# One added wait on the load queue of a two-layer attention and mixture-of-experts kernel

## The reference

```python
for l in range(DEPTH):                      # DEPTH = 2
    h = rmsnorm(x, norm_attn[l])
    proj = h @ w_in[l]                      # 1024 x 6336, float32
    ...                                     # three attentions out_a, out_b, out_c
    x = x + mixed.astype(x.dtype) @ w_out[l]
    x = x + hier_moe(rmsnorm(x, norm_ffn[l]), ...)   # silu(t @ w_gate) * (t @ w_up), then @ w_down
return rmsnorm(x, norm_final)
```

## Time and profile before

| | us |
|---|---|
| median of 3 runs | 1009.46 (1009.01 to 1010.76) |
| profiled execution, its own time | 1008.15 |
| its span, first to last instruction | 1006.4 |
| what lies around the span | 1.75 |
| PE busy | 931.0 (93%) |
| the first layer's last right half lands | 497.1 |
| barrier between the layers passed | about 503.6 |

### The profile page before, as it was taken

How to read it: one execution, slowest core, us unless ns; L and a number is a source line. 1 busy time by engine, 2 the same in 40 slices (tenths; PEclk the granted TensorE clock), 3 DMA queues, 4 the chain that set the end, 5 groups by cost and what they waited for, 6 DMA issues and landing times. The chain is left out here.

```text
span 1006.4 us, 13781 instructions
## 1 busy us (share of the span) xinstructions
PE 931.0 (93%) x5372; PEld 613.1 (61%) x5372; DVE 409.6 (41%) x1068; ACT 244.2 (24%) x688; POOL 78.8 (8%) x122
## 2 busy tenths in 40 slices
PE   9999999999999998677899999999999999986676
PEld 8888778775455543334288887887744655531242
DVE  2523676774773211111131337677557621110112
ACT  2211454552111020000111015655411202000002
POOL 0300000104000000000030000000230000000000
PEclk9999999999999999898999999999999999997898
DMA  9985655429889999999998443436398899999995
GB/s 284 302 277 146 145 168 156 168 96 320 336 345 371 421 421 421 421 421 421 363 326 272 136 148 110 142 100 215 123 363 331 340 397 420 420 421 421 421 417 202
DMA packets 133206, 295.06 MB, mean 293 GB/s; under 512 B 14142, under 2 KB 93076, under 8 KB 111636
## 3 DMA queue, kind: packets, MB, share of 16 engines
q1 hardware_dynamic: 128832, 289.41, 77.5%
q10 hardware_dynamic: 4308, 4.75, 2.5%
HBM read 291.50 MB, written 2.64 MB: 292 GB/s over the span
## 5 line engine op out<-in xcount | busy, mean ns | idle before, releaser
L1307 PE MATMUL bank<-ring,tail 128*128 128x256 f32 x672 | 156.2, 383 | 0.2
L2323 PE MATMUL bank<-ring,tail 128*32 128x512 f32 x896 | 112.4, 659 | 47.1 <-DMA ring<-in_moe_w_up 43.1
L1307 PEld LDWEIGHTS bank<-ring,tail 128*128 128x128 f32 x672 | 124.2, 190 | 24.5 <-issue 8.3
L1112 PE MATMUL bank<-tail,ring 128*128 128x256 f32 x512 | 112.6, 380 | 0.0
L2323 PEld LDWEIGHTS bank<-ring,tail 128*32 128x32 f32 x896 | 32.9, 120 | 122.4 <-issue 122.1
L1112 PEld LDWEIGHTS bank<-tail,ring 128*128 128x128 f32 x512 | 96.7, 190 | 13.4 <-issue 0.4
L2669 DVE SCALAR_TENSOR_TENSOR tail<-tail,bank 128x256 f32<-128x256 f32 x16 | 6.7, 421 | 229.5 <-ACT tail L2481 229.5
L1647 ACT ACTIVATE ring<-ring,small 128x128 f32<-128x128 f32 (+1 forms) x128 | 56.6, 443 | 77.5 <-DVE small L1953 77.5
L1469 PE MATMUL bank<-ring,tail 128*128 128x512 f32 x168 | 73.6, 593 | 0.0
L2380 PE MATMUL bank<-ring,tail 128*32 128x512 f32 x480 | 61.5, 623 | 5.6 <-DVE tail L2682 3.6
L2330 PE MATMUL bank<-tail 128*128 128x512 f32 x128 | 59.2, 605 | 0.0
(11 more groups left out here) (350 smaller groups left out, 1205.6 us busy)
## 6 DMA issues: line engine op xcount, KB each, us to landing
ring<-in_moe_w_up SPq DMA_DIRECT2D x56, 1024.0 KB, 21.8
ring<-in_moe_w_gate SPq DMA_DIRECT2D x56, 1024.0 KB, 19.7
ring<-in_moe_w_down SPq DMA_DIRECT2D x52, 1024.0 KB, 14.4
ring<-in_w_in SPq DMA_DIRECT2D x47, 1024.0 KB, 9.5
ring<-in_w_out SPq DMA_DIRECT2D x8, 1024.0 KB, 8.1
ring<-in_moe_w_down SPq DMA_DIRECT2D x16, 512.0 KB, 16.2
ring<-in_moe_w_gate SPq DMA_DIRECT2D x14, 512.0 KB, 9.5
ring<-in_moe_w_up SPq DMA_DIRECT2D x14, 512.0 KB, 9.5
```

The costliest lines, as they stand in the source:

```text
L1112: last = pe.matmul(dst, weight(k), hT[:, k, :], start=(k == 0), stop=(k == KD - 1))
L1307: last = pe.matmul(dst, tokens[:, k, :], weights[:, k, :], start=False, stop=(k == KD // 2 - 1), skip_group_check=True)
L2323: last = pe.matmul(bank[4][CAP * e:CAP * e + CAP, :].rearrange("p (a f) -> p a f", a=2), XT[:, k, CAP * e:CAP * e + CAP], ring[:, lo:hi + ...
```

## The change

One wait is added in `moe_sync`, behind the issues of the eight down halves and ahead of all that follows them on SP. It stands in both layers. No load is added, taken away or put in another order.

```diff
                 down_half(sp, layer, c, 0, landed[moe_slot(c)])
             for c in range(LOADS - 4, LOADS):
                 down_half(sp, layer, c, 1, s_side)
+            sp.wait_ge(s_side, layer * 112 + 112)
             if layer + 1 < DEPTH:
                 sp.wait_ge(s_gu, NGRP - 1)
                 for n in range(EARLY):
```

## The result

The changed kernel takes 1012.92 us at the median of 8 runs (1011.10 to 1016.08), the kernel before 1009.48 (1008.66 to 1011.03) beside it: a ratio of 1.0034 with a 95% interval of 1.0023 to 1.0044, or 3.4 us. (A ratio here is the one measured over the runs and need not be exactly that of the two medians beside it.) A second set of 12 runs of the same kernel gave 1012.44 against 1009.72, 1.0026 (1.0016 to 1.0037). The profiled execution took 1012.67 us with a span of 1010.9, against 1008.15 and 1006.4.

The account below looks back on a forecast made before the run. It took a layer to be PE-bound in attention and bound by the weight stream in its experts. SP's lateness of 1.0 and the clock's 1.4 gave +2.4 on 1009.46, so 1011.9 us, range 1009.4 to 1013.0.

Parts of the forecast that it names:

- SP at the barrier: Seam of the layers: SP's last load issue ends after VectorE, opening the barrier 1.0 us later, bounds 0 to 2.
- SP in time: Rival at the seam: VectorE still opens the barrier, price 0, 1009.2 to 1009.5 us; chance 0.17.
- The clock: Behind the seam: the PE's hole of 2.6 us lowers the clock on line 1218, 1.4 us, bounds 0 and some 1.8.
- The sum: Whole kernel: 0 - 0 + 1.0 + 1.4 = +2.4 us, so 1011.9 for the median; chance 0.48.
- What the change might give: Group 7's down: an earlier right half saves at most 0.24 us of PE wait; 0 was taken.
- The readers: Second layer's attention: loads land about 2.3 us later but before they are read, so their readers don't notice.
- the last layer: Final norm's weights held until 991.5, in by 996.8, ahead of VectorE's read: cost 0, slack 2 us or more.
- The clock holding: Rival at the seam: the longer hole costs only itself, +1.0 us, 1010.5; chance 0.26.
- rival 3: Larger loss: lines 535 and 536 drain slowly or loads reach readers late, 1 to 2 us on top, 1013.5; chance 0.06.

Follow-up runs that it names:

- experiment 3: Against experiment 1: attention loads 2 and 3 of the second layer issued behind the barrier instead of ahead; 1009.14 us against 1010.13 before, 0.9996.
- experiment 4: Against experiment 1: only attention load 3 of the second layer issued behind the barrier; 1009.81 us against 1009.34 before, 1.0001.
- experiment 1: Against the changed kernel: the added wait stands in the first layer alone; 1012.99 us against 1010.13 before, 1.0021.
- the second kernel with idle matmuls: The changed kernel plus 20 idle matmuls on the PE behind the first layer's last scatter; 1012.10 us, 1.0017.
- experiment 7: 20 idle matmuls on the PE behind the first layer's last scatter, added to experiment 1 (1011.93 us, 1.0019), then to the changed kernel (1012.10, 1.0017).
- experiment 5: Against the changed kernel: in both layers SP waits for the last left half instead of the last right one; 1009.33 us against 1009.34 before, 1.0003.
- the second pair: The changed kernel run again (1012.44 us, 1.0026) beside it with 20 idle matmuls behind the first layer's last scatter (1012.10, 1.0017).
- the first kernel with idle matmuls: Against experiment 1: 20 idle matmuls on the PE behind the first layer's last scatter; 1011.93 us against 1010.13 before, 1.0019.
- experiment 2: Against the kernel before: the wait added in the last layer alone; 1009.36 us against 1010.13, 0.9995.
- experiment 6: Against the kernel before: wait in the first layer only, with attention load 0 issued ahead of it; 1009.93 us against 1009.34, 1.0009.

## Why the prediction was right, and where it was off

**SP at the barrier: right, and undersized.** That SP's 1.5 us of slack are the whole slack of the place, that load 2's issue ends with load 0's landing, and that load 3's issue then brings SP in behind VectorE, all stands in the rows (502.87 and 503.0; 505.06). Experiments 3 and 4 show it to be the cause. The term was put at 1.0 us, bounds 0 to 2. It measured 2.2, 1.8 and 1.3 by the PE's idle time ahead of line 1101 (3.81, 3.42 and 2.86 instead of 1.60) in the three profiled executions (the changed kernel, experiment 1, the second set) of kernels with all four loads ahead of the barrier and no idle matmuls. Two figures in it were small. Load 0 was to take 5.3 us on an idle queue, by the earlier trace rows; it took 6.4, 6.0 and 5.5. The row's load was alone, and here others follow at once, but that isn't enough of an explanation: with the same loads behind it load 0 took 5.3 in the second kernel with idle matmuls. It does go with the issue of the small transfer of line 536: in the seven executions that issue load 0 to an empty queue, this issue lasted 1.3 to 1.4 us where load 0 took 5.3 to 5.5, and 1.9, 2.4 and 2.6 us where it took 6.0, 6.4 and 6.8. Which of the two makes the other long is open. And SP's step from load 0's landing to its last issue's end was 2.1 instead of 1.8.

The estimate of 4.4 us for load 0 from the Trainium skill ("DMA: Bandwidth & Descriptors", section Anatomy of one DMA) was the other case, SP in time. The Trainium skill gives that sum for the path of transfers that GpSimd issues, and the prediction applied it to one of SP's without saying so. No run here bears it out: with load 0 at the head of an idle queue it took 5.3 us at the least.

**The clock: right, on a weak row.** It fell in all three of those executions, and cost 1.7, 1.5 and 1.7 by the time from the PE's start to line 1118, where 1.4 was forecast. Its price at the level of whole runs is less clear (experiment 7). The reading that a hole of 2.6 us would lower it rested on one place, the holes of 1.41 and 1.00 us with 0.51 of work between. The same place in the other profiled executions shows how little one execution tells: after 1.4 and 1.0 to 1.2 us the clock fell there in four executions (before, experiment 5, and both kernels of the second pair in experiment 7) and stayed up in four (experiments 1, 3 and 4 and the first kernel with idle matmuls). In the remaining four executions the PE was late from an earlier fall, and the second hole was missing or short. Nor was the hole near 474 one of 1.63 us: that is its share of the window, the whole hole was 2.02:

```profile
476.39 7.07 PE L2323 MATMUL bank<-ring,tail 128*32 128x512 f32 x64 [2.02 <-issue]
```

So the step from 1.60 to 2.6 us was in part a guess that came true. The upper bound of 1.8 us had no row either; 1.7 comes close to it.

**The sum.** 1.0 + 1.4 = 2.4 was forecast, 3.4 and 2.7 measured in two sets. The forecast of 1011.9 is 1.0 below the first median. In that kernel's profile the missing part is SP's term (2.2 instead of 1.0) and 0.3 of the clock's; in the second profiled execution each of the two is 0.3 over its forecast.

**What the change might give: the conclusion right, the bound wrong.** The bound of 0.24 us for the PE's wait on the right half was read from the only two places of the profile of before, and in both the clock had fallen in down of group 6, which made the PE late for the half. With the full clock there the PE waits 0.6 to 1.3 us in the first layer and up to 2.4 in the last. An earlier landing would have been worth that much. It didn't come: the half took 11.2 to 11.3 us from issue to landing with nothing behind it and 11.4 to 11.5 with a load behind it, so at most 0.3 us were gained.

**The readers, the last layer:** as forecast. Loads that land 2.7 to 5 us later cost nothing (experiment 3: load 0 at 502.8 instead of 500.1, load 2 at 510.6 instead of 505.7), and neither does the wait in front of the final norm's weights (experiment 2), which took 3.5 us where under 5.3 was said.

**The rivals.** The clock holding and SP in time stayed away in the changed kernel; the second is what experiments 3 to 6 bring about on purpose. Of rival 3 the late readers stayed away; its other half, a slow drain of lines 535 and 536 from an empty queue, may be what made load 0 late, as said above. The range held both medians, but the first, 1012.92, lies only 0.1 us inside its end of 1013.0, and half of its eight runs lie beyond that. That the range held there is in part luck.

## What to carry to other kernels

An issue of a transfer is work of the engine that issues it, and it can block (here it lasted 2 to 5 us on a full queue, instead of 0.4); before a wait is put ahead of a row of issues, find the next barrier behind them and read how long ahead of the others that engine comes there now. If loads are to be held back, issue only so many ahead of the barrier as go through before the others come to it, and the rest behind it. And an idle time read from one execution is no bound where the clock fell just ahead of it: read it in an execution in which the clock stayed up as well.

## What the runs showed of the hardware

- With pieces of 1 KB, SP's issue of load 2, the third load of about 1 MB on the queue, returned just when load 0 landed, within 0.3 us: 502.87 and 502.99 in the changed kernel, 502.06 and 502.11 in experiment 4, 499.48 and 499.54 in experiment 5. Load 3's issue, where it stands ahead of the barrier, ended 1.8 to 2.1 us after that landing (3.5 in one kernel with idle matmuls). In experiment 1 load 2's issue at 499.68 and load 3's took 5.10 us together, against some 0.4 us for an issue that isn't held.
- The first layer's last right half landed 11.2 to 11.3 us after its issue with nothing queued behind it and 11.4 to 11.5 with loads queued behind it: they slowed it by 0.3 us or less.
- A hole of the PE of 2.9 to 3.8 us was followed by the lower clock in three executions of three, one of 1.5 to 1.9 us at the seam by none in nine. In the last layer, ahead of the right half's matmuls, holes of 2.2 and 2.4 us (experiments 4 and 1) were followed by it and holes of 1.6 to 2.0 us in five other executions weren't. Near 471 and 474 two holes follow one another with 2.9 us of matmuls between: 1.9 to 2.1 us and then 2.0 were followed by it in four executions of four, 0.7 to 1.4 and then 2.0 in none of eight. At the seam the same work took 1.5 to 1.7 us more with a stretch at the lower level in it.
- Issue to landing of the last right half of the last layer varied from 11.3 to 12.8 us, also between kernels that are alike there (11.3 in experiment 3, 12.4 in experiment 1). It was 11.3 to 11.6 in four of the five executions with the clock low in that layer's down of group 6 (before and experiments 3, 5 and 6), and 12.2 to 12.8 in the fifth (the first kernel with idle matmuls) and in the seven others. What makes it vary is open, and it moves the end of the program by more than several of the effects measured here.
